# The third copy of probabilities on ScalarE, moved behind the second exponentials in dense heads that have a next one

## The chip, the core and the metric

The kernel runs on one core of one Trainium2 chip. The metric is the device time of one execution in microseconds; the time given is the median of the runs shown. Everything is computed in fp32, with matmuls of large operands split into a high and a low part.

## What is computed

A bidirectional encoder of two layers. Each layer projects its input (1,040 tokens, 1,024 channels) with `w_in`, runs three groups of mixers beside one another (a windowed attention A, two pairs of gated recurrences C0 and C1, four dense heads B0 to B3), projects with `w_out`, adds and normalises. The change lies in the dense heads, which are a differential attention:

```python
def attend(q_blk):                       # one block of 128 queries, c = 0, 1
    s = einsum('bqhcd,bkhcd->bhcqk', q_blk, k) * scale
    s = where(key_ok, s, NEG)
    p = softmax(s, axis=-1)
    a = p[:, :, 0] - lam * p[:, :, 1]
    return einsum('bhqk,bkhv->bqhv', a, v)
...
ob = rms_norm(ob, subln_w) * (1.0 - lam_init)
yb = ob * silu(gb)
```

Each head and query block has two score rows (c = 0 and 1) over 1,040 keys, two softmaxes, and a weighted difference that multiplies the values.

## The kernel before

All five engines run instruction streams written out by hand, which meet in semaphores; nothing schedules them but their order in the code. PSUM has eight banks, and `bank_plan` (line 240) gives every product its bank in advance. `filled` and `released` semaphores count the uses of each bank: `wait_filled` waits until TensorE has written a use, `wait_read` and `wait_free` until the reader has let it go.

The tokens are nine blocks: eight of 128 and the last, number 8, of the 16 meta tokens. Layer 0 needs all nine blocks as queries (`q_tiles` = 9), layer 1 eight.

The dense heads run in four passes a layer (`pass_b`, once for each engine: line 1100 for TensorE, 1431 for ScalarE, 1898 for VectorE), one pass a head, one step a query block. The passes of B0, B1 and B2 have a next head `nx`: its queries and keys are projected in halves of 12 matmuls between the work of the present head. B3 has none. The lists of `b_steps` (line 211) say which half products each step holds. In layer 0 the pass of B0 has two each in steps 0 and 1, one each in steps 2 to 5 and none in 6 to 8; those of B1 and B2 have two each in steps 0 to 5 and none in 6 to 8. In layer 1 the pass of B0 has two each in steps 0 to 2, one in 3 and 4, none in 5 to 7; those of B1 and B2 have three each in steps 0 and 1, two in 2 to 4, none in 5 to 7.

A step t of a pass goes like this. `after` is the next step, which at the end of a head is the first one of the next head.

- TensorE (lines 1151 to 1168): the scores of `after` into banks 2 to 5 (line 996), a wait for the combination of t, nine transposes of the combined p in three groups of three (line 1127; groups 0 and 2 into bank 0, group 1 into bank 1), a half product behind groups 0 and 1 and one behind group 2 if there are any (line 856), the values for key blocks 0 to 5, the values for blocks 6 to 8 (line 1143, into bank 1). The values for blocks 6 to 8 wait for the third copy. In the last step but one of a pass with a next head the meta scores of the next head follow (line 1085, matmuls of line 996).
- ScalarE (lines 1477 to 1497): two copies of transposed p out of PSUM, `evac_probs` 0 and 1 (line 1451), the exponentials of `after` for c = 0 (`exps`, a small one at line 1439 and the large one at line 1441, which also frees the score banks), the third copy `evac_probs` 2 (line 1451), the exponentials for c = 1, the output of the values (`values_out`, line 1461), and the normalisation (lines 1468 to 1472). In some steps a copy of rotated queries and keys of the next head stands among them (`qk_hi_of`, line 1419): that of pieces 0 and 1 ahead of the first exponentials, that of the last piece, in the last step but one, just ahead of the second.
- VectorE (lines 1942 to 1957): the maxima of `after` for c = 0 and 1 (lines 1906 and 1907), low parts of the next head (`qk_lo`, line 1881), its rotary work (`qk_rope`, lines 1867 to 1873), the end of the step before (`finish`), and the combination of `after` (`combine`, lines 1916 to 1922), which needs both exponentials.
- SyncE moves rotated pieces and saves results; GpSimd splits weights beside a maximum.

What the numbers in the prediction rest on is this order and three waits of the code:

```python
pe.wait_ge(b_comb, B_STEP[l, g, t])               # 1153, before the transposes
wait_read(pe, ("aT", l, g, t, k // 3))            # 1141, before values 0, 3, 6
pe.wait_ge(qk_lo_done, QK_PIECE[l, g, "qk", len(T_PIECES) - 1])   # 1088, meta scores
```

Scores also wait for their banks, that is for the exponentials of the step before (line 1111).

Of the kernel before, what the change touches and what calls it, by code (L numbers as in the profile page):

```python
# [62 lines left out]
def rows(t):  # L63
    return META if t == MT else P


def q_tiles(l):

    return TILES if l < DEPTH - 1 else REAL
# [141 lines left out]
def b_steps(l, nx):  # L211


    n = q_tiles(l)
    halves = [(u, half) for u in (units(l, nx, "qk") if nx else []) if u not in early(nx) for half in range(2)]
    q, r = divmod(len(halves), n - 3)
    ends = [(t + 1) * q + min(t + 1, r) for t in range(n)]
    parts = [halves[a:b] for a, b in zip([0] + ends, ends)]
    turned = [[]] + [[u for u, half in p if half] for p in parts[:-1]]
    rounded = [[] for _ in range(n)]  # L220
    rounded[0] += [j for f, j in early(nx) if f]
    for t in range(n):
        for f, j in turned[t]:
            if f:
                rounded[min(t + 2, n - 2)].append(j)
    return [(t, parts[t], turned[t], rounded[t]) for t in range(n)]
# [7 lines left out]
def b_step(l, g, t, k):  # L234
    steps = [(h, u) for h in B_HEADS for u in range(q_tiles(l))]
    i = steps.index((g, t)) + k
    return steps[i] if 0 <= i < len(steps) else None
# [183 lines left out]
def build(nc, x, meta, emb_ln_g, emb_ln_b, w_in, w_out, a_sink, b_lam, c_lb_logits, norm_cols,  # L421
# [177 lines left out]
    def slot_of(g):  # L599
        return (head_no(g) + 1) % 2  # L600

    def bank(key):
        return BANK[key][0]
# [6 lines left out]
    def wait_filled(eng, key):  # L610
        b, n = BANK[key]
        eng.wait_ge(filled[b], n + 1)

    def wait_read(eng, key):
        b, n = BANK[key]
        eng.wait_ge(released[b], n + 1)
# [584 lines left out]
    def _(act):  # L1201
        n_sca = [0]

        def then(ins):
            n_sca[0] += 1
            ins.then_inc(sca, 1)
            act.wait_ge(sca, n_sca[0])

        def hi_of_rows(what, l, t):
            for j in range(2):  # L1210
                key = (what, l, t, j)
                wait_filled(act, key)
                nc.scalar.copy(h_rows(hT_hi, j, t),
                               psum[:, bank(key), :].rearrange("p (k c) -> p k c", k=4)[:, :, 0:rows(t)]).then_inc(hi_split, 1)
# [201 lines left out]
        def qk_hi_of(l, g, j):  # L1416
            a, n = T_PIECES[j]
            act.wait_ge(qk_placed, 16 * 4 * QK_PIECE[l, g, "qk", j])
            nc.scalar.copy(qk_b[:, slot_of(g), 0:2, a:a + n], qk_t[:, :, 0:n]).then_inc(qk_hi, 1)

        def meta_out(l, g):
            for c in range(2):
                key = ("meta", l, g, c)
                n = q_tiles(l)
                wait_filled(act, key)
                if n == TILES:
                    nc.scalar.copy(meta_s[0:META, slot_of(g), c, MT, :], psum[0:META, bank(key), MT * META:TILES * META])
                nc.scalar.copy(meta_s[:, slot_of(g), c, 0:REAL, :].rearrange("p t m -> p (t m)"),
                               psum[:, bank(key), 0:REAL * META]).then_inc(released[bank(key)], 1)

        def pass_b(l, g, nx):
            def exps(step, c):
                g, t = step
                n = B_STEP[l, g, t]
                m, i = rows(t), n % 2
                act.wait_ge(b_max, B_COMP[l, g, t, c])
                b = bank(("s", l, g, t, c))
                probs = p0_b[0:m, i] if c == 0 else p1_b[0:m]
                nc.scalar.activation(probs[:, REAL * P:TOK], meta_s[0:m, slot_of(g), c, t, :], ACT.Exp, scale=SCALE,
                                     bias=neg_max[0:m, i, c:c + 1], accum_out=row_sum[0:m, i, 2 * c + 1:2 * c + 2])  # L1440
                nc.scalar.activation(probs[:, 0:REAL * P].rearrange("p (i n) -> p i n", i=2), psum[0:m, b:b + 2, :],  # L1441
                                     ACT.Exp, scale=SCALE, bias=neg_max[0:m, i, c:c + 1],
                                     accum_out=row_sum[0:m, i, 2 * c:2 * c + 1]).then_inc(released[b], 1)

            def evac_probs(t, j):
                key = ("aT", l, g, t, j)
                b, m = bank(key), rows(t)
                wait_filled(act, key)
                if b_step(l, g, t, -1) and j == 0:
                    wait_filled(act, ("o", l, *b_step(l, g, t, -1)))  # L1450
                nc.scalar.copy(aT_b[:, 3 * j:3 * j + 3, 0:m],  # L1451
                               psum[:, b, 0:3 * P].rearrange("p (k c) -> p k c", k=3)[:, :, 0:m])\
                    .then_inc(released[b], 1)

            def values_out(t):
                key = ("o", l, g, t)
                n, b = B_STEP[l, g, t], bank(key)
                wait_filled(act, key)
                if n > 2:
                    act.wait_ge(b_y, n - 2)  # L1460
                nc.scalar.copy(o_b[0:rows(t), n % 2, :], psum[0:rows(t), b, 0:P]).then_inc(released[b], 1)

            def norm(step):
                g, t = step
                n, m = B_STEP[l, g, t], rows(t)
                wait_read(act, ("o", l, g, t))
                act.wait_ge(b_scale, n)
                then(nc.scalar.activation(b_junk[0:m, :], o_b[0:m, n % 2, :], ACT.Square,
                                          accum_out=sumsq[0:m, t, 0:1]))
                then(nc.scalar.activation(rstd[0:m, t, 0:1], sumsq[0:m, t, 0:1], ACT.Ln, bias=eps_rms[0:m],  # L1470
                                          scale=fscale[0:m, n % 4, :]))
                nc.scalar.activation(rstd[0:m, t, 0:1], rstd[0:m, t, 0:1], ACT.Exp, scale=-0.5).then_inc(rstd_ready, 1)

            if g == "B0":
                exps((g, 0), 0)
                exps((g, 0), 1)
            for t, _, _, before in b_steps(l, nx):
                after = b_step(l, g, t, 1)
                evac_probs(t, 0)
                evac_probs(t, 1)  # L1480
                for j in before:
                    if j < len(T_PIECES) - 1:
                        qk_hi_of(l, nx, j)
                if after:
                    exps(after, 0)
                evac_probs(t, 2)
                for j in before:
                    if j == len(T_PIECES) - 1:
                        qk_hi_of(l, nx, j)
                if after:  # L1490
                    exps(after, 1)
                values_out(t)
                norm((g, t))
                if nx and t == q_tiles(l) - 2:
                    meta_out(l, nx)
                if not nx and t >= Y_LAG:
                    hi_of_rows("y", l, t - Y_LAG)
# [5 lines left out]
        for l in range(DEPTH):  # L1503
# [32 lines left out]
            for g, nx in b_passes(l):  # L1536
                pass_b(l, g, nx)
# [526 lines left out]
```

## Time and profile before

| | |
|---|---|
| median of 3 runs | 1895.43 us (1888.45 to 1899.31) |
| the profiled execution | 1886.95 us, span 1885.6 us |
| granted TensorE clock, mean | 0.965 of full speed |
| busy: TensorE | 1707.6 us (91%) |
| busy: VectorE | 1100.9 us (58%) |
| busy: ScalarE | 886.8 us (47%) |
| busy: GpSimd | 402.9 us (21%) |
| chain that ended last | TensorE 70%, VectorE 16%, ScalarE 6% |

The busy shares are means over stages with different limits. The dense heads take some 300 us in each layer (562 to 858 and 1481 to 1776 us of the span). A timeline row gives the start, the length, the engine, the line, the operation with what it writes and reads, and in brackets the idle time of the engine before it and what ended it. Matmuls are pipelined, so their rows overlap: the distance of two starts says more than a length.

### The profile page before, as it was taken

Reading aid. Unit: us, or ns where it says so; the run is one execution under the profiler, and the core shown is the slowest. Engines: PE = TensorE matmul, PEld = TensorE weight load, DVE = VectorE, ACT = ScalarE, POOL = GpSimd, SP = SyncE. Lnnn points to the kernel's source line nnn. Section 1 sums busy time; section 2 is a strip of 40 time slices with the busy share of each in tenths; the row PEclk is TensorE's granted clock in tenths of the full one; section 3 lists DMA queues with packets and bytes.
Section 4 is the critical chain, followed back from the end, with each engine's and each line's share of the span. In section 5 each row is a group of like instructions: output and inputs, shape, how many; then the busy total and the mean of one; then the engine's idle time right before and its main releaser. Section 6 shows DMA issues by size and latency. Waiting matters only on the chain.

```text
span 1885.6 us, 35772 instructions
## 1 busy us (share of the span) xinstructions
PE 1707.6 (91%) x13754; PEld 1584.6 (84%) x13754; DVE 1100.9 (58%) x2533; ACT 886.8 (47%) x2652; POOL 402.9 (21%) x390
## 2 busy tenths in 40 slices
PE   3799999999998999989989989999998898888896
PEld 2798899999887788768989989999998878776796
DVE  6585584345537777783185845834453575667616
ACT  4434545345506666682063344452553374647603
POOL 5430221220111002011373103113103001012044
PEclk9999999999989999899999999999998999899998
DMA  7200100200020111142121001012001111103312
GB/s 256 69 24 13 57 23 27 77 23 13 32 78 15 38 31 38 46 143 96 37 103 53 24 14 56 23 34 70 26 13 59 50 29 31 47 22 128 121 46 90
DMA packets 97705, 102.44 MB, mean 54 GB/s; under 512 B 7488, under 2 KB 87600, under 8 KB 97280
## 3 DMA queue, kind: packets, MB, share of 16 engines
q1 hardware_dynamic: 96576, 99.08, 16.3%
q8 instruction: 111, 1.82, 0.4%
q10 hardware_dynamic: 960, 1.07, 0.2%
q14 instruction: 58, 0.48, 0.1%
HBM read 70.43 MB, written 21.17 MB: 49 GB/s over the span
## 4 chain that ended last, share of the span: by engine, by line
PE 70%; DVE 16%; ACT 6%; POOL 3%; issue 2%; DMA 2%; SPq 0%; DVEq 0%; ACTq 0%
PE psum L856 45%; PE psum L996 7%; PE psum L931 3%; PE psum L1143 3%; PE psum L1050 3%; DVE row_max L1906 3%; PE psum L1127 2%; ACT p_b L1441 2%; DVE p_b L1920 2%; PE psum L1036 1%; POOL w_lo L822 1%; PE psum L903 1%; ACT aT_b L1451 1%; PE psum L979 1%; PE psum L974 1%
## 5 line engine op out<-in xcount | busy, mean ns | idle before, releaser
L856 PE MATMUL psum<-w_hi,hT_hi 128*128 128x256 f32 x1824 | 529.2, 290 | 6.2 <-POOL w_lo L822 4.3
L856 PE MATMUL psum<-w_hi,hT_lo 128*128 128x256 f32 x1824 | 516.6, 283 | 0.0
L856 PE MATMUL psum<-w_lo,hT_hi 128*128 128x256 f32 x1824 | 516.3, 283 | 0.0
L818 POOL CAST w_hi<-w_raw 128x512 fp32r<-128x512 f32 (+1 forms) x168 | 109.6, 652 | 1319.4 <-DMA w_raw<-in_w_in 791.5
L856 PEld LDWEIGHTS psum<-w_hi,hT_hi 128*128 128x128 f32 x1824 | 347.6, 191 | 14.8 <-POOL w_lo L822 5.1
L856 PEld LDWEIGHTS psum<-w_hi,hT_lo 128*128 128x128 f32 x1824 | 347.5, 191 | 0.0
L856 PEld LDWEIGHTS psum<-w_lo,hT_hi 128*128 128x128 f32 x1824 | 347.4, 190 | 0.0
L856 PE MATMUL psum<-hT_hi,w_hi 128*128 128x346 f32 (+1 forms) x672 | 229.8, 342 | 24.6 <-DVE hT_lo L1565 9.3
L856 PE MATMUL psum<-hT_hi,w_lo 128*128 128x346 f32 (+1 forms) x672 | 220.9, 329 | 0.0
L856 PE MATMUL psum<-hT_lo,w_hi 128*128 128x346 f32 (+1 forms) x672 | 220.6, 328 | 0.0
L822 POOL TENSOR_TENSOR w_lo<-w_raw,w_hi 128x512 fp32r<-128x512 f32 (+1 forms) x168 | 211.4, 1258 | 25.9 <-DVE neg_max L1907 14.1
L1906 DVE TENSOR_REDUCE row_max<-psum 128x1 f32<-128x1024 f32 x136 | 165.8, 1219 | 54.5 <-PE psum L996 54.5
L1143 PE MATMUL psum<-vg_b,aT_b 128*128 128x128 f32 (+1 forms) x1224 | 164.9, 288 | 5.0 <-ACT aT_b L1451 4.4
L996 PE MATMUL psum<-qk_b 64*128 64x512 f32 (+2 forms) x1224 | 144.4, 372 | 22.6 <-ACT p_b L1441 18.1
L1143 PEld LDWEIGHTS psum<-vg_b,aT_b 128*128 128x128 f32 (+1 forms) x1224 | 149.5, 192 | 13.7 <-ACT aT_b L1451 8.5
L856 PEld LDWEIGHTS psum<-hT_hi,w_hi 128*128 128x128 f32 x672 | 131.3, 195 | 27.0 <-issue 10.0
L1441 ACT ACTIVATE p_b<-psum,neg_max 128x1024 f32<-128x1024 f32 x136 | 149.9, 1102 | 0.0
L996 PEld LDWEIGHTS psum<-qk_b 64*128 64x128 f32 (+1 forms) x1224 | 101.3, 193 | 46.0 <-issue 25.0
L1451 ACT COPY aT_b<-psum 128x384 f32<-128x384 f32 (+1 forms) x204 | 88.2, 464 | 108.2 <-PE psum L1127 106.2
L856 PEld LDWEIGHTS psum<-hT_hi,w_lo 128*128 128x128 f32 x672 | 131.4, 196 | 0.0
L856 PEld LDWEIGHTS psum<-hT_lo,w_hi 128*128 128x128 f32 x672 | 130.7, 194 | 0.0
L1127 PEld LDWEIGHTS psum<-ident,p_b 128*128 128x128 f32 (+1 forms) x612 | 70.9, 149 | 64.0 <-DVE p_b L1920 30.8
(161 smaller groups left out, 2618.6 us busy)
## 6 DMA issues: line engine op xcount, KB each, us to landing
w_raw<-in_w_in SPq DMA_DIRECT2D x72, 256.0 KB, 3.5
w_raw<-in_w_in SPq DMA_DIRECT2D x28, 512.0 KB, 4.2
h_dram<-hbuf SPq DMA_DIRECT2D x16, 512.0 KB, 2.6
w_raw<-in_w_out SPq DMA_DIRECT2D x16, 512.0 KB, 4.1
hbuf<-h_dram SPq DMA_DIRECT2D x16, 512.0 KB, 5.9
qk_b<-y_dram SPq DMA_DIRECT2D x16, 512.0 KB, 3.2
y_dram<-y_stage SPq DMA_DIRECT2D x96, 64.0 KB, 1.6
qk_t<-rot SPq DMA_DIRECT2D x56, 86.5 KB, 2.1
```

What stands on the lines that cost most here:

```text
L818: pool.tensor_copy(hi, raw).then_inc(w_hi_done, 1)
L822: pool.tensor_tensor(lo, raw, hi.bitcast(F32), ALU.subtract).then_inc(w_split, 1)
L856: last = nc.tensor.matmul(out_ap, lhs[a](k), rhs[b](k), start=k == 0 and a + b == 0, stop=k == KT - 1 and b == 1)
L931: last = nc.tensor.matmul(o_ap, k_sel[p0:p0 + HD, a:a + m], q_ap, start=True, stop=True)
L996: last = [nc.tensor.matmul(out_of(r), q_of(a, r), k_of(b, r), start=i == 0, stop=i == 2) for r in range(2)]
L1050: last = nc.tensor.matmul(psum[0:m, bank(o_key), h * HD:(h + 1) * HD], pT_a[:, h % 2, j, 0:m], v_a[:, f + j - 1 if j else MT, v0:v0 + HD], ...
L1127: last = nc.tensor.transpose(psum[:, b, i * P:i * P + m], p0_b[0:m, B_STEP[l, g, t] % 2, k * P:(k + 1) * P], ident[0:m, 0:m])
L1143: last = nc.tensor.matmul(psum[0:m, b, 0:P], aT_b[:, k, 0:m], vg_b[:, head_no(g), k, 0:P], start=k == 0, stop=k == TILES - 1)
L1441: nc.scalar.activation(probs[:, 0:REAL * P].rearrange("p (i n) -> p i n", i=2), psum[0:m, b:b + 2, :], ACT.Exp, scale=SCALE, bias=neg_max[ ...
L1451: nc.scalar.copy(aT_b[:, 3 * j:3 * j + 3, 0:m], psum[:, b, 0:3 * P].rearrange("p (k c) -> p k c", k=3)[:, :, 0:m])\
L1906: then(nc.vector.tensor_reduce(row_max[0:m, i, c:c + 1], psum[0:m, b:b + 2, :], AX.XY, ALU.max))
L1920: stt(p0_b[0:m, i, 0:TOK], p1_b[0:m, :], coef[0:m, j, 0:1], p0_b[0:m, i, 0:TOK], ALU.mult, ALU.add).then_inc(b_comb, 1)
```

## The change

In a pass that has a next head, the third copy of the transposed probabilities (`evac_probs(t, 2)`) is issued after the exponentials for c = 1 of the next step instead of between those for c = 0 and c = 1. In the pass of B3 it stays where it was.

```diff
@@ -1483,12 +1483,16 @@
                         qk_hi_of(l, nx, j)
                 if after:
                     exps(after, 0)
-                evac_probs(t, 2)
+                if not nx:
+                    evac_probs(t, 2)
                 for j in before:
                     if j == len(T_PIECES) - 1:
                         qk_hi_of(l, nx, j)
                 if after:
                     exps(after, 1)
+                if nx:
+
+                    evac_probs(t, 2)
                 values_out(t)
                 norm((g, t))
                 if nx and t == q_tiles(l) - 2:
```

On ScalarE a common step of such a pass, before (p_b is the buffer of probabilities, aT_b that of the transposed ones):

```order
L1451 COPY aT_b<-psum 128x384 x2
L1439 ACTIVATE p_b,row_sum<-meta_s,neg_max 128x16
L1441 ACTIVATE p_b,row_sum<-psum,neg_max 128x1024
L1451 COPY aT_b<-psum 128x384
L1439 ACTIVATE p_b,row_sum<-meta_s,neg_max 128x16
L1441 ACTIVATE p_b,row_sum<-psum,neg_max 128x1024
L1461 COPY o_b<-psum 128x128
```

and with the change:

```order
L1451 COPY aT_b<-psum 128x384 x2
L1439 ACTIVATE p_b,row_sum<-meta_s,neg_max 128x16
L1441 ACTIVATE p_b,row_sum<-psum,neg_max 128x1024
L1439 ACTIVATE p_b,row_sum<-meta_s,neg_max 128x16
L1441 ACTIVATE p_b,row_sum<-psum,neg_max 128x1024
L1451 COPY aT_b<-psum 128x384
L1461 COPY o_b<-psum 128x128
```

The copy of 128x384 that stood between the two pairs of exponentials now stands behind both, just ahead of the output of the values.

The last step but one of a pass, on ScalarE (here in the pass of B0 in layer 0, where `after` has 16 rows), before:

```order
L1451 COPY aT_b<-psum 128x384 x2
L1439 ACTIVATE p_b,row_sum<-meta_s,neg_max 16x16
L1441 ACTIVATE p_b,row_sum<-psum,neg_max 16x1024
L1451 COPY aT_b<-psum 128x384
L1419 CAST qk_b<-qk_t 128x2x346
L1439 ACTIVATE p_b,row_sum<-meta_s,neg_max 16x16
L1441 ACTIVATE p_b,row_sum<-psum,neg_max 16x1024
L1461 COPY o_b<-psum 128x128
```

and with the change:

```order
L1451 COPY aT_b<-psum 128x384 x2
L1439 ACTIVATE p_b,row_sum<-meta_s,neg_max 16x16
L1441 ACTIVATE p_b,row_sum<-psum,neg_max 16x1024
L1419 CAST qk_b<-qk_t 128x2x346
L1439 ACTIVATE p_b,row_sum<-meta_s,neg_max 16x16
L1441 ACTIVATE p_b,row_sum<-psum,neg_max 16x1024
L1451 COPY aT_b<-psum 128x384
L1461 COPY o_b<-psum 128x128
```

The copy of rotated queries and keys (line 1419) now follows the first exponentials at once, and the third copy has moved behind two instructions more. The rows of TensorE, VectorE, GpSimd and SyncE stand as before.

## Rows read from the trace of the kernel before

**Rows 1.** The waits, whole run: engine line <- releaser: us in total, times, longest us
```profile
PEld psum L1127 <- DVE p_b L1920: 30.8, 31, 2.9
```

**Rows 2.** Timeline, a full step (B1, layer 0): start us, us, engine, line, operation
```profile
659.85 0.88 PE L1127 MATMUL psum<-ident,p_b 128*128 128x128 f32 x6
...
659.96 1.22 DVE L1906 TENSOR_REDUCE row_max<-psum 128x1 f32<-128x1024 f32 x1 [1.50 <-PE psum L996]
...
661.41 0.31 ACT L1439 ACTIVATE p_b<-meta_s,neg_max 128x16 f32<-128x16 f32 x1
...
662.54 0.29 DVE L1907 SCALAR_TENSOR_TENSOR neg_max<-row_max,meta_max 128x1 f32<-128x1 f32 x1
...
664.70 2.17 PE L1143 MATMUL psum<-vg_b,aT_b 128*128 128x128 f32 x18
...
666.81 1.67 PE L996 MATMUL psum<-qk_b 64*128 64x512 f32 x12
...
668.40 0.87 PE L1127 MATMUL psum<-ident,p_b 128*128 128x128 f32 x6
...
668.50 1.23 DVE L1906 TENSOR_REDUCE row_max<-psum 128x1 f32<-128x1024 f32 x1 [1.20 <-PE psum L996]
```

**Rows 3.** Timeline, half steps 3 and 4 of B0, layer 0
```profile
597.36 0.87 PE L1127 MATMUL psum<-ident,p_b 128*128 128x128 f32 x6 [0.62 <-DVE p_b L1920]
...
598.73 0.31 ACT L1439 ACTIVATE p_b<-meta_s,neg_max 128x16 f32<-128x16 f32 x1
...
600.87 0.31 ACT L1439 ACTIVATE p_b<-meta_s,neg_max 128x16 f32<-128x16 f32 x1
...
604.48 0.87 PE L1127 MATMUL psum<-ident,p_b 128*128 128x128 f32 x6 [0.32 <-DVE p_b L1920]
...
611.86 0.87 PE L1127 MATMUL psum<-ident,p_b 128*128 128x128 f32 x6 [0.32 <-DVE p_b L1920]
```

**Rows 4.** Timeline, bare steps 5 and 6 of B0, layer 1
```profile
1533.35 0.87 PE L1127 MATMUL psum<-ident,p_b 128*128 128x128 f32 x6 [0.32 <-DVE p_b L1920]
...
1538.47 0.15 DVE L1916 TENSOR_TENSOR inv_sum<-row_sum 128x2 f32<-128x2 f32 x1
...
1540.47 0.88 PE L1127 MATMUL psum<-ident,p_b 128*128 128x128 f32 x6 [0.69 <-DVE p_b L1920]
...
1541.85 0.31 ACT L1439 ACTIVATE p_b<-meta_s,neg_max 128x16 f32<-128x16 f32 x1
...
1543.24 0.46 ACT L1451 COPY aT_b<-psum 128x384 f32<-128x384 f32 x1
...
1543.60 0.77 ACT L1419 CAST qk_b<-qk_t 128x692 fp32r<-128x692 f32 x1
...
1543.76 0.94 PE L1143 MATMUL psum<-vg_b,aT_b 128*128 128x128 f32 x6 [0.18 <-ACT aT_b L1451]
...
1544.27 0.31 ACT L1439 ACTIVATE p_b<-meta_s,neg_max 128x16 f32<-128x16 f32 x1
...
1545.34 2.85 PE L996 MATMUL psum<-qk_b 64*128 64x16 f32 x48 [0.65 <-DVE qk_b L1881]
```

**Rows 5.** Timeline, bare step 7 of B0, layer 1
```profile
1553.41 0.32 ACT L1439 ACTIVATE p_b<-meta_s,neg_max 128x16 f32<-128x16 f32 x1
...
1555.02 0.16 DVE L1916 TENSOR_TENSOR inv_sum<-row_sum 128x2 f32<-128x2 f32 x1 [1.94 <-ACT p_b L1441]
...
1557.03 0.88 PE L1127 MATMUL psum<-ident,p_b 128*128 128x128 f32 x6 [0.30 <-DVE p_b L1920]
```

**Rows 6.** Stretches, end of B2, layer 0: length, busy PE PEld DVE ACT POOL, PEclk, DMA, GB/s
```profile
775.00:780.00 5.00, 3.09 (x25) 1.65 (x24) 4.65 (x13) 2.74 (x9) 0.00 (x0) 1.00 0.32 72
...
785.00:790.00 5.00, 5.00 (x44) 4.45 (x44) 2.38 (x10) 0.74 (x5) 0.00 (x0) 0.50 0.01 4
```

**Rows 7.** The chain of waits, meta scores and scores at two head ends: start us, us
```profile
630.94 4.93 PE psum L996 x66
...
783.55 7.03 PE psum L996 x51
```

## The prediction

> **What bounds the kernel now.** I write a step of a dense head as the time from T, the start of TensorE's first six transposes of p (line 1127), to the next such start. The change acts in the 51 steps that have a next head: 27 of layer 0, 24 of layer 1. I split them by how many half products of the next head's queries and keys TensorE has in them, as the lists of `b_steps` give it: 27 *full* steps (two or three), 6 *half* steps (one: steps 2 to 5 of B0 in layer 0, steps 3 and 4 of B0 in layer 1), and 18 *bare* steps (none: the last three of each of six passes). Read first the waits: TensorE's weight load before the transposes waits for VectorE's combination 31 times [rows 1]. That is under half of the 68 steps of both layers, so most steps are bound by TensorE and some by the softmax chain. Then I read the timeline of one step of each kind.
>
> Full step [rows 2]: transposes at 659.85 (the step before it ended there), next at 668.40, 8.55 us, with no wait printed on TensorE. The reader is to see that the second maximum is out at 662.83 (662.54+0.29) and that the values begin at 664.70 and the next scores at 666.81.
>
> Half step [rows 3]: 597.36 to 604.48, 7.12 us. First exponentials start at 598.73 (T+1.37), second at 600.87, and TensorE then waits for line 1920.
>
> Bare steps [rows 4]: 1533.35 to 1540.47, also 7.12 us; the next one ends in the meta scores at 1545.34, which wait for the low parts (line 1881). The last step of a head [rows 5] goes from the second exponentials (1553.41) by the combination (1555.02) to the next transposes (1557.03).
>
> **The change, part by part.** One copy of 128x384 (line 1451) moves behind one pair of exponentials. No instruction is added, none removed, no DMA is touched, and TensorE, VectorE, GpSimd and SyncE keep their order. What moves is who comes first on ScalarE. Behind it three things hang: the last three matmuls of the values (k = 6 to 8), bank 0, and by TensorE's own order the next scores or the meta scores. The normalisation follows the values and is late with them, but VectorE asks for it only behind the two maxima of the next step, and SyncE for the result only after that.
>
> *Gain.* Between the start of the copy and the start of what follows it lie 0.36 us (1543.24 to 1543.60) [rows 4]. Where the copy also waited for TensorE's transposes, as in the half step, the second exponentials can start at T+1.37+1.39 = T+2.76 instead of T+3.51: 0.75 us earlier. The 1.39 is what one pair of exponentials holds ScalarE (1541.85 to 1543.24) [rows 4].
>
> *Cost.* From the start E of the second exponentials there are two ways to the next transposes. By the combination: 1.61 + 2.01 = E+3.62 [rows 5]. By TensorE, new: the copy starts at E+1.39, the last values 0.52 later (1543.24 to 1543.76) [rows 4], they take a third of 664.70 to 666.81, 0.70, and the scores 1.59 (666.81 to 668.40) [rows 2]. That is E+4.20. So once the copy stands behind the exponentials, TensorE's way is the longer by 0.58 us, and what E gains must first pay for that. Also, if scores and not the combination set T, the first maximum starts 0.10 behind T (668.40, 668.50), and the first exponentials 1.45 behind the maximum (659.96 to 661.41) [rows 2]: at T+1.55 instead of T+1.37.
>
> By kind:
> - Full steps, 27: ScalarE is free at 661.41+1.39 = 662.80 and the maximum is there at 662.83; the copy then starts at 664.22, and block 6 is ready at 664.74. TensorE comes to it after twelve of eighteen matmuls, at 664.70+1.40 = 666.10 [rows 2]. Slack 1.4 us, or 0.7 where a copy of 0.67 (line 1419) comes first. Nothing changes: 0. The earlier combination is worth nothing either, since no TensorE instruction of the step waits for it; if the cover of 1.4 us were gone, each such step would pay the overrun.
> - Half steps, 6: after the first, T+1.55+1.39+4.20 = T+7.14 against 7.12, so 0.02 each. The two with a copy of line 1419 ahead: 1.37+0.67+1.39+4.20 = 7.63 against 604.48 to 611.86, 7.38 [rows 3]: +0.25 each. Together +0.6.
> - First bare step of a head, 6: the combination starts at 1538.47 with no idle time printed ahead of it [rows 4], so VectorE's own rotary work holds it either way and the step keeps its length; only in B0, where the half steps before have shifted the maximum by 0.18, it moves: 2 x 0.18 = +0.4.
> - Second bare step, 6, up to the meta scores. Before: 1540.47 to 1545.34 = 4.87. After: 1.37+1.39 = 2.76 the copy of line 1419, +0.67 the second exponentials, +1.39 the moved copy, +0.52+0.70 the values, so the meta scores at 6.04. The low parts, which ended the wait before, would be ready earlier and no longer matter. +1.17 each, and meta scores, scores and maximum follow one another without a gap, so it goes to the end: +7.0.
> - Third bare step, 6: E is 0.36 earlier, then 4.20 instead of 3.62: +0.22 each [rows 4, 5], +1.3.
> - The first step of B3, unchanged in itself, inherits the late maximum: 2 x 0.17 = +0.3.
>
> Sum +9.6 us.
>
> *The clock*, which the steps above take as full. After the bare steps of B2 in layer 0 TensorE, busy 3.09 of 5 us, has 1.00 granted at first, then 0.50 in 785 to 790 (the level of 1.2 GHz), and the meta scores with the scores take 7.03 us there against 4.93 at the end of B0 [rows 6, 7]. The change adds idle time just ahead of that place in six heads. Bounds: nothing, if none of the six is slower than before, and 6 x 2.1 = 12.6. I take one more slow crossing, 2.1, since of the two crossings shown one is slow already [rows 7].
> The Trainium skill, page "TensorE: Matmul & The Clock Gate", section "Loop structure matters more than you think", says that another engine copying a result out of PSUM doesn't break the clock. By that rule this term is nil and the sum is 9.6; the rows speak against relying on it, since the clock fell in a stretch where TensorE's waits are of just this sort.
>
> Total +11.7, say +12. The profiled execution took 1886.95 us, 8.5 below the median of the three runs; both move by the same sum, so 1899 for such an execution and **1907.4 us** for the median.
>
> **The rivals.**
> - *The clock carries it.* The added idle makes most of the six crossings run at half clock: 9.6 + 12.6 = +22, 1917.6 us. For it: the two levels and their prices [rows 6, 7]. Against: stretches of bare steps now stay at 1.00 for several us.
> - *Half of it is hidden.* If the meta scores' delay is taken up behind them (the last step of a head waits for its own maxima too), half of the 7.0 goes: +6, 1901 us, not to be told from no change, since under about 0.5% (9.5 us) a measurement of this kernel sees nothing. Against: the transposes of that step follow the scores at once.
> - *The earlier combination wins*, the other side. Place: half and bare steps. If TensorE's way from E were no longer than 3.62, each gets what E gains: 4 x 0.75 and 2 x 0.36 in half steps, 6 x 0.36 in third bare steps, 6 x 0.36 at the meta scores, in all 8.1 us less, 1887.3; up to -10 if the rotary steps gain. It decides where the copy starts before E+0.81 instead of E+1.39. Against it: ScalarE is in order and a pair holds it 1.39 us. For it: only that a trace's waits are inferred.
> - *The copy in full steps is late.* With 0.3 us over in each it would be +8 more. Against: the slack of 1.4.
>
> **How the numbers follow.** Forecast (+9.6 to +14): 0.50, of which 0.10 falls under 9.5. Clock: 0.15. Half hidden, some +3 to +8: 0.25, of which 0.02 over the line. Combination wins: 0.10, half of it beyond 0.5%. The late copy in full steps is counted with the clock case. Slower 0.57, same 0.38, faster 0.05. The range from 1897 (+2) to 1920 (+25) leaves out the winning combination and what is beyond six slow crossings.
>
> **What would show it.** Right: in bare steps the copy of line 1451 starts 1.39 behind the second exponentials, TensorE's wait for it before the last values grows to about 1 us and more, the waits for line 1920 before the transposes nearly vanish, the meta scores start 6.0 behind T and wait for the values, and full steps stay at 8.55. Wrong: if full steps grow, if half steps fall under 7.0, or if the meta scores still wait for line 1881.

## The result, and the profile after

The changed kernel took 1922.95 us (median of 4 runs, 1919.51 to 1929.96), the kernel before 1892.93 us (4 runs). The ratio is 1.016 with a 95% interval of 1.0131 to 1.0189: 30 us slower, where +12 was forecast and 1920 (+25) was the end of the range. When it was measured once more it was 1.0149 (1.0125 to 1.0173). The profiled execution took 1929.96 us and is the slowest of its four, while that of the kernel before (1886.95 us) is faster than all of its four; so the two traces lie 43 us apart, not 30.

The page of the changed kernel (busy times; the granted clock in 40 slices; the chain by engine):

```profile
span 1928.6 us, 35772 instructions
...
PE 1733.7 (90%) x13754; PEld 1602.8 (83%) x13754; DVE 1099.4 (57%) x2533; ACT 888.7 (46%) x2652; POOL 403.3 (21%) x390
...
PEclk9899999999989898899999999999998899898998
...
PE 72%; DVE 14%; ACT 8%; POOL 2%; issue 2%; DMA 2%; SPq 0%; DVEq 0%; ACTq 0%
```

TensorE has 26 us more of busy time for the same 13,754 matmuls: they ran slower, not more often. The stage table says where; 12.8 and 4.7 us of the 26 lie in its second and fourth rows. It cuts the span at the first transposes of the dense heads and at those of B3, in each layer; the columns are the length, the busy times of PE, PEld, DVE, ACT and POOL with their counts, the granted clock, the DMA share and GB/s. Before:

```profile
0.00:572.61 572.61, 505.19 (x4215) 477.89 (x4215) 315.37 (x791) 246.17 (x754) 134.49 (x133) 0.97 0.18 57
572.61:797.20 224.59, 210.42 (x1601) 182.90 (x1599) 169.90 (x377) 149.95 (x453) 25.94 (x27) 0.95 0.12 32
797.20:1491.85 694.65, 649.25 (x5357) 612.64 (x5357) 377.05 (x875) 289.48 (x870) 165.75 (x162) 0.98 0.17 55
1491.85:1721.72 229.87, 204.86 (x1466) 181.79 (x1465) 153.69 (x332) 135.88 (x399) 25.86 (x27) 0.92 0.12 32
1721.72:1885.60 163.88, 137.90 (x1120) 129.38 (x1120) 84.85 (x162) 65.33 (x176) 50.88 (x41) 0.96 0.29 103
```

After:

```profile
0.00:579.39 579.39, 510.83 (x4214) 483.66 (x4214) 316.14 (x791) 246.47 (x754) 134.51 (x133) 0.96 0.18 56
579.39:821.57 242.18, 223.21 (x1602) 191.50 (x1600) 170.12 (x376) 150.23 (x453) 25.98 (x27) 0.90 0.12 32
821.57:1519.39 697.82, 652.25 (x5359) 614.21 (x5358) 374.26 (x874) 289.97 (x870) 165.96 (x162) 0.97 0.17 54
1519.39:1764.58 245.19, 209.60 (x1466) 184.23 (x1464) 154.05 (x331) 136.60 (x399) 25.92 (x27) 0.91 0.11 31
1764.58:1928.60 164.02, 137.85 (x1122) 129.17 (x1120) 84.85 (x161) 65.45 (x176) 50.93 (x41) 0.96 0.29 102
```

The reader is to see the second and fourth rows, the passes that the change touches: 224.59 to 242.18 us and 229.87 to 245.19 us, +32.9 together, at a granted clock of 0.95 to 0.90 and 0.92 to 0.91. (In layer 1 the mean clock hardly differs, because the trace of before was slow in other places of that row; the steps below say more.) The other three rows, which hold the same instructions in the same order, are 10.1 us longer in this pair of executions (6.8 of it ahead of the first dense head). The first row differs so without the change too: full_steps_only, below, has 578.69 us there in its profiled execution and is no slower than the kernel before.

The waits of the changed kernel that answer to [rows 1] come second; the first line is from the kernel before:

```profile
PEld psum L1143 <- ACT aT_b L1451: 8.5, 18, 1.0
```

```profile
PEld psum L1143 <- ACT aT_b L1451: 43.8, 31, 2.6
...
PEld psum L1127 <- DVE p_b L1924: 17.1, 17, 2.9
...
PE psum L996 <- DVE qk_b L1885: 0.9, 2, 0.5
```

The wait before the transposes fell from 30.8 us in 31 cases to 17.1 in 17. Of these 17, 11 lie in the passes of B3, which the change leaves alone (13 before); elsewhere it fell from 18 cases to 6. In its place stands the wait of the values for the third copy, 43.8 us in 31 cases where it was 8.5 in 18. The meta scores wait for the low parts (line 1881, now 1885) in two places only.

A half step after, step 3 of B0 in layer 0, to be held against [rows 3]:

```profile
605.29 0.87 PE L1127 MATMUL psum<-ident,p_b 128*128 128x128 f32 x6
...
606.81 0.31 ACT L1439 ACTIVATE p_b<-meta_s,neg_max 128x16 f32<-128x16 f32 x1
...
608.28 0.31 ACT L1439 ACTIVATE p_b<-meta_s,neg_max 128x16 f32<-128x16 f32 x1
...
609.67 0.47 ACT L1451 COPY aT_b<-psum 128x384 f32<-128x384 f32 x1
...
610.19 0.94 PE L1143 MATMUL psum<-vg_b,aT_b 128*128 128x128 f32 x6 [0.46 <-ACT aT_b L1451]
...
611.05 1.65 PE L996 MATMUL psum<-qk_b 64*128 64x512 f32 x12
...
612.64 0.87 PE L1127 MATMUL psum<-ident,p_b 128*128 128x128 f32 x6
```

First exponentials at T+1.52, second at T+2.99 (T+3.51 before), the copy 1.39 behind them, the last values 0.52 later, the scores 0.86 later, the next transposes 1.59 later: 7.35 us against 7.12. A full step keeps its length, and its values have no wait:

```profile
682.08 0.87 PE L1127 MATMUL psum<-ident,p_b 128*128 128x128 f32 x6
...
686.49 0.47 ACT L1451 COPY aT_b<-psum 128x384 f32<-128x384 f32 x1
...
686.91 2.17 PE L1143 MATMUL psum<-vg_b,aT_b 128*128 128x128 f32 x18
...
690.61 0.87 PE L1127 MATMUL psum<-ident,p_b 128*128 128x128 f32 x6
```

The second bare step of B0 in layer 1, with what follows (to be held against [rows 4, 5]):

```profile
1568.23 0.87 PE L1127 MATMUL psum<-ident,p_b 128*128 128x128 f32 x6
...
1569.78 0.31 ACT L1439 ACTIVATE p_b<-meta_s,neg_max 128x16 f32<-128x16 f32 x1
...
1571.83 0.31 ACT L1439 ACTIVATE p_b<-meta_s,neg_max 128x16 f32<-128x16 f32 x1
...
1573.23 0.47 ACT L1451 COPY aT_b<-psum 128x384 f32<-128x384 f32 x1
...
1573.74 0.94 PE L1143 MATMUL psum<-vg_b,aT_b 128*128 128x128 f32 x6 [2.41 <-ACT aT_b L1451]
...
1574.61 7.10 PE L996 MATMUL psum<-qk_b 64*128 64x16 f32 x60
...
1581.64 1.28 PE L1127 MATMUL psum<-ident,p_b 128*128 128x128 f32 x6
...
1586.63 0.94 PE L1143 MATMUL psum<-vg_b,aT_b 128*128 128x128 f32 x6 [1.54 <-ACT aT_b L1451]
```

The meta scores start 6.38 us behind T, where they started at 4.87. Then the meta scores and scores take 7.03 us to the next transposes (1574.61 to 1581.64), where they took 4.36 (1545.34 to 1549.70). So this step is 4.18 us longer, 1.51 by the wait and 2.67 by slower matmuls.

The prediction calls the meta scores with the scores behind them a *crossing*, from one head to the next. TensorE is busy without a break in it, so its length shows the clock alone. In layer 0 it has 66 matmuls. Here is that of B2 in the kernel before, in the changed kernel, and in full_steps_only (below), where this step has the order of the kernel before:

```profile
783.55:790.49 6.94, 6.94 (x66) 5.90 (x66) 3.57 (x15) 2.10 (x11) 0.00 (x0) 0.59 0.03 9
804.76:812.82 8.06, 8.06 (x68) 7.01 (x67) 1.92 (x10) 1.80 (x9) 0.00 (x0) 0.50 0.00 0
792.56:796.91 4.35, 4.35 (x66) 3.81 (x67) 3.14 (x13) 2.10 (x11) 0.00 (x0) 1.00 0.05 15
```

The same work takes 4.35 us at full clock and 8.06 at half. The six crossings together take 32.4 us in the kernel before, at granted clocks of 0.59 to 0.97, and 45.0 us in the changed one, at 0.50 to 0.60. At full clock throughout they would take 25.9 (three of 4.35 and three of 4.27 us).

### The profile page after: what moved, and what is told of

It is laid out like the page before. It is cut to its first block, busy times and chain, and to the rows that moved or that the text cites. A ratio compares the mean times of both kernels' runs of the same rounds, so it can differ in the third digit from the quotient of the medians.

```text
span 1928.6 us, 35772 instructions
## 1 busy us (share of the span) xinstructions
PE 1733.7 (90%) x13754; PEld 1602.8 (83%) x13754; DVE 1099.4 (57%) x2533; ACT 888.7 (46%) x2652; POOL 403.3 (21%) x390
## 4 chain that ended last, share of the span: by engine, by line
PE 72%; DVE 14%; ACT 8%; POOL 2%; issue 2%; DMA 2%; SPq 0%; DVEq 0%; ACTq 0%
PE psum L856 44%; PE psum L996 9%; PE psum L1143 4%; PE psum L931 3%; ACT p_b L1441 3%; DVE row_max L1910 3%; PE psum L1050 3%; PE psum L1127 2%; PE psum L1036 1%; DVE hbuf L1583 1%; ACT aT_b L1451 1%; PE psum L903 1%; DVE stats L1576 1%; ACT p_b L1439 1%; POOL w_lo L822 1%
## 5 line engine op out<-in xcount | busy, mean ns | idle before, releaser
L1143 PEld LDWEIGHTS psum<-vg_b,aT_b 128*128 128x128 f32 (+1 forms) x1224 | 147.8, 189 | 49.5 <-ACT aT_b L1451 43.8
L996 PE MATMUL psum<-qk_b 64*128 64x512 f32 (+2 forms) x1224 | 165.1, 410 | 14.1 <-ACT p_b L1441 13.2
L996 PEld LDWEIGHTS psum<-qk_b 64*128 64x128 f32 (+1 forms) x1224 | 115.9, 228 | 41.0 <-issue 19.3
```

The costliest lines, as they stand in the source:

```text
L996: last = [nc.tensor.matmul(out_of(r), q_of(a, r), k_of(b, r), start=i == 0, stop=i == 2) for r in range(2)]
L1143: last = nc.tensor.matmul(psum[0:m, b, 0:P], aT_b[:, k, 0:m], vg_b[:, head_no(g), k, 0:P], start=k == 0, stop=k == TILES - 1)
```

## The experiments

Two theories stood against one another. The **wait theory**: a wait costs its length, as in the prediction's sum. The **clock theory**: the longer idle time of TensorE at the end of a pass brings the granted clock down to 0.50 over the meta scores and scores, and most of the loss is that. The table has the length of the six *meta steps* in each kernel's trace (second bare step, from transposes to transposes), in the order B0, B1, B2 of layer 0, then of layer 1. Each row of six comes from one traced execution, while the median comes from 4 to 12 runs. Each ratio is to the kernel before measured beside it, whose medians were 1891.58 to 1894.06 us after the first one of 1892.93:

| kernel | six meta steps, us | sum | median, us | ratio to before, 95% |
|---|---|---|---|---|
| before | 9.69 10.46 11.77 9.23 10.76 9.64 | 61.6 | 1892.93 | |
| changed | 13.51 13.92 14.43 13.41 14.10 13.96 | 83.3 | 1922.95 | 1.0160 (1.0131 to 1.0189) |
| changed_again | 13.50 14.12 14.63 13.55 14.31 14.20 | 84.3 | 1923.36 | 1.0149 (1.0125 to 1.0173) |
| full_steps_only | 11.47 10.64 9.19 9.73 9.65 9.93 | 60.6 | 1892.78 | 0.9993 (0.9977 to 1.0009) |
| only_meta_step | 12.37 12.77 13.18 12.53 14.90 13.21 | 79.0 | 1909.41 | 1.0091 (1.0059 to 1.0123) |
| all_but_meta_step | 11.00 11.86 11.62 10.56 11.72 11.93 | 68.7 | 1909.11 | 1.0081 (1.0053 to 1.0109) |
| filled_wait | 10.60 13.49 10.99 10.66 10.51 12.56 | 68.8 | 1910.86 | 1.0093 (1.0063 to 1.0124) |
| filled_wait_again | 10.60 13.50 10.98 13.26 10.82 10.81 | 70.0 | 1918.55 | 1.0136 (1.0115 to 1.0158) |
| filled_wait_nine | 10.61 11.11 12.94 10.66 11.33 11.22 | 67.9 | 1907.64 | 1.0086 (1.0065 to 1.0108) |
| bare_steps_filled | 11.96 11.73 11.38 10.63 10.64 13.29 | 69.6 | 1907.59 | 1.0094 (1.0069 to 1.0120) |
| only_meta_filled | 10.94 12.91 10.52 11.65 12.21 12.08 | 70.3 | 1908.11 | 1.0083 (1.0061 to 1.0104) |
| only_meta_filled_nine | 10.92 10.52 11.55 12.14 10.48 10.49 | 66.1 | 1902.19 | 1.0051 (1.0032 to 1.0069) |
| high_parts_first | 9.78 10.51 11.89 9.59 9.45 9.72 | 60.9 | 1893.15 | 1.0006 (0.9993 to 1.0019) |
| before_filled | 11.38 10.57 9.19 9.92 10.05 10.18 | 61.3 | 1893.51 | 1.0015 (1.0000 to 1.0030) |

A single step says little: that of B2 in layer 0, with the order of the kernel before, took 11.77, 9.19, 11.89 and 9.19 us in four of these kernels. The sums of six with that order and nothing moved near them agree: 61.6, 60.6, 60.9 and 61.3.

### Which of the moves cost: full_steps_only, only_meta_step, all_but_meta_step

In the kernel before, `late` says in which steps the copy moves:

```diff
+                late = nx and len(halves) > 1             # full_steps_only
+                late = nx and t == q_tiles(l) - 2         # only_meta_step
+                late = nx and t != q_tiles(l) - 2         # all_but_meta_step
-                evac_probs(t, 2)
+                if not late:
+                    evac_probs(t, 2)
...
                     exps(after, 1)
+                if late:
+                    evac_probs(t, 2)
```

> The copy is moved only in the 27 steps with two or three half products. Both theories: TensorE reaches the last values 1.4 us after the copy is done, so nothing, 1893 within 0.3%. If the copy were late in full steps, each would be longer than 8.55 us and this kernel slower by more than 5 us.

Measured: 0.9993. The 27 full steps cost nothing, as the slack in [rows 2] said, and the rival of a late copy in full steps is out.

> The third copy is moved only in the step that ends in the meta scores (6 steps), 45 of the moves are undone. Wait theory (an added wait costs its length and no more): +7.0 us by the prediction's sum, near 1900. Clock theory (the wait ahead of the meta scores leaves them, and what follows, at half clock): the six steps now cost 21.8 us and the steps behind them some 4 more, so +20 to +26 us, 1913 to 1919, and the meta step is 13.5 us long in layer 0 against 9.7.

Measured: 1.0091, 17 us for six moves, where the waits alone should have made 7. The six steps take 79.0 us in place of 61.6, which is those 17 us. Half of it, 8.7 us, lies in the crossings (41.1 us in place of 32.4); the other half is the later start of the meta scores, 1.32 to 1.36 us in five of the six steps and not 1.17.

> The copy is moved in 45 steps and stays between the exponentials in the six that end in the meta scores. Wait theory: +2.6 us, no change that can be told, 1896. Clock theory: the meta scores start without the long wait, so most crossings keep the clock they have in the kernel before: +3 to +8 us, 1896 to 1901. If the idle time of the bare steps in general is what lowers the clock, the crossings stay slow and it comes out at +15 or more, 1908.

Measured: 1.0081, 15 us for 45 moves that should have made 2.6. This was above what either theory had named, and at the level that the expectation gave for idle time of the bare steps in general. In the trace the first and third bare steps are 3.8 and 2.9 us longer, the half steps 1.4. The six meta steps have the order of the kernel before, and yet they are 7.1 us longer in sum: 1.1 us before the meta scores start, 6.0 us in the crossings (38.4 us in place of 32.4). The second one of them (length, busy times, granted clock 0.75):

```profile
712.63:724.49 11.86, 10.82 (x93) 9.11 (x93) 7.06 (x21) 6.35 (x21) 0.00 (x0) 0.75 0.10 24
```

So matmuls ran slower in steps whose own order is unchanged. More idle time ahead of them is not the reason: the meta step and the step ahead hold 20.3 us of TensorE's idle time over the six heads, and 20.2 and 20.3 in full_steps_only and high_parts_first. What differs is how it is spread. The waits of the first bare step of B2 in layer 0, in the kernel before and then in all_but_meta_step:

```profile
774.54 0.94 PE L1143 MATMUL psum<-vg_b,aT_b 128*128 128x128 f32 x6 [0.82 <-ACT aT_b L1451]
...
776.03 1.57 PE L996 MATMUL psum<-qk_b 64*16 64x512 f32 x12 [0.55 <-ACT p_b L1441]
...
778.72 0.88 PE L1127 MATMUL psum<-ident,p_b 128*128 128x128 f32 x6 [1.12 <-DVE p_b L1920]
```

```profile
788.09 0.94 PE L1143 MATMUL psum<-vg_b,aT_b 128*128 128x128 f32 x6 [2.20 <-ACT aT_b L1451]
...
790.87 0.88 PE L1127 MATMUL psum<-ident,p_b 128*128 128x128 f32 x6 [0.36 <-DVE p_b L1924]
```

Three waits of 0.82, 0.55 and 1.12 us have become one of 2.20 and one of 0.36, and the step is as long as before (8.09 us). That the long wait is what lowers the clock in the next step is argued from this; no run varies it alone. Both halves of the change lose by themselves, and their losses add up to about the whole (17 + 15 against 30).

### Filling the wait with work: filled_wait, filled_wait_again, filled_wait_nine, changed_again

The changed kernel, with products added that nobody reads, ahead of the last values in the six meta steps. They go to the bank that the meta scores overwrite next. Only work is added.

```diff
+                if nx and t == q_tiles(l) - 2:
+                    for c in range(2):
+                        wait_free(pe, ("meta", l, nx, c))
+                    for _ in range(7):                    # 9 in filled_wait_nine
+                        nc.tensor.matmul(psum[0:rows(t), bank(("meta", l, nx, 0)), 0:P], aT_b[:, 0, 0:rows(t)],
+                                         vg_b[:, head_no(g), 0, 0:P], start=True, stop=True)
                 values(t, range(6, TILES))
```

> The changed kernel with seven products of values added in the six meta steps, written into the bank of the meta scores while TensorE waits for the third copy: 1.6 us of work inside a wait of 2.2 us, whose results nobody reads. Wait theory: the work is hidden and the time stays at the changed kernel's 1923. Clock theory: the meta scores and scores keep full clock, 4.9 us instead of 6.9, in six places, and it comes down by 10 to 15 us, 1908 to 1913.

Measured: 1910.86, 12 us below the changed kernel with more work to do. Two of the six meta steps stayed slow, 13.49 and 12.56 us. The meta step of B0 in layer 1: before, then changed, then filled_wait.

```profile
1540.47:1549.70 9.23, 8.16 (x87) 6.83 (x87) 6.74 (x17) 6.29 (x19) 0.00 (x0) 0.98 0.12 30
```

```profile
1568.23:1581.64 13.41, 10.76 (x90) 9.11 (x88) 6.83 (x17) 6.46 (x19) 0.00 (x0) 0.78 0.09 21
```

```profile
1555.88:1566.54 10.66, 9.56 (x103) 8.42 (x101) 6.83 (x17) 6.46 (x19) 0.00 (x0) 1.00 0.11 28
```

The three clocks are 0.98, 0.78 and 1.00, the lengths 9.23, 13.41 and 10.66 us. At full clock the change costs this step 1.43 us; what lies above that, 2.75 us, is the clock at its lower level of 1.2 GHz for part of the step.

> filled_wait once more, with more rounds, since only_meta_filled did not gain as it should. Clock theory: again 10 us or more below the changed kernel's 1923, 1907 to 1913. Wait theory: 1923.

Measured: 1918.55, 1.0136 (1.0115 to 1.0158). That is only 4 us below the changed kernel's median, where ten were expected, and the intervals overlap: a miss. Its trace has two slow meta steps (13.50 and 13.26 us), as the one of filled_wait had; why the medians differ by 8 us is not shown. Seven products do not keep the clock reliably.

> The changed kernel itself, beside the next one on the same chip, since the two fillings of seven came to 1910.9 and 1918.6 in different jobs. Both theories: 1.016 of the kernel before, 1920 to 1926, and 13 to 14.5 us for each meta step.

> The changed kernel with nine products of values as filler in the wait of the six meta steps, 2.1 us at full clock in a wait of 2.2. Wait theory: equal to changed_again. Clock theory: at least 8 us below changed_again, 1906 to 1914, and at least four of the six meta steps at 10.5 to 11 us with a granted clock of 0.95 or more. What then remains over the kernel before, 13 to 20 us, is the waits themselves (12 us by the steps at full clock) and slow stretches in the other bare steps.

These two ran on the same chip. Measured: 1923.36, with meta steps of 13.50 to 14.63 us, and 1907.64. Nine products in each of six waits make the kernel 15.7 us faster. All six meta steps are shorter than in changed_again, by 16.4 us in sum. But only two of them, not four, came to 10.5 to 11 us at a clock of 0.95 or more; the other four were granted 0.93, 0.76, 0.93 and 0.94, so this part of the expectation was wrong. The steps of B0 in layer 1 and of B2 in layer 0, the fast one and the one that stays slow:

```profile
1554.23:1564.89 10.66, 10.01 (x108) 8.87 (x106) 6.82 (x17) 6.46 (x19) 0.00 (x0) 1.00 0.11 28
788.49:801.43 12.94, 12.77 (x114) 10.97 (x112) 7.14 (x20) 6.54 (x21) 0.00 (x0) 0.76 0.07 19
```

### Filling elsewhere: only_meta_filled, only_meta_filled_nine, bare_steps_filled, before_filled

The first two are only_meta_step with the same filler of seven and of nine products.

> The copy is moved only in the six meta steps, and the wait that this makes is filled with seven products of values that nobody reads. Wait theory: the filler changes nothing, so it stays at the 1909.4 of the unfilled one. Clock theory: with full clock over the meta scores what is left is the wait itself, 6 x 1.2 = +7, 1900 to 1902, and the meta steps are 10.6 us long in layer 0.

Measured: 1908.11 against 1909.41, no gain that can be told, though in the profiled executions the six steps went from 79.0 to 70.3 us. A miss of the clock theory as put. In five of the six the clock is still under 1, here the fourth:

```profile
1555.56:1567.21 11.65, 10.73 (x102) 9.09 (x102) 6.74 (x17) 6.40 (x19) 0.00 (x0) 0.89 0.10 25
```

> The copy moved in the six meta steps alone and nine products as filler instead of seven, 2.1 us at full clock in a wait of 2.2. With seven it came to 1908.1 against 1909.4 without any, and the granted clock in five of the six steps was still 0.80 to 0.95. Clock theory: with the wait closed the steps come near 10.6 us and the time to 1902 or less. If it stays at 1908, the filler inside this wait is not what decides here, and the idle time of the steps ahead sets the clock; in filled_wait those steps are in the other order.

Measured: 1902.19, 1.0051 (1.0032 to 1.0069). With the wait closed the loss is 9.6 us instead of the 17 of the unfilled kernel, and four of six steps are at 10.5 to 10.9. So the filler does decide here, and seven were too few; against only_meta_filled alone the intervals still touch.

bare_steps_filled is the changed kernel with fillers of five, seven and six products in the three bare steps, each ahead of the last values. `idle_work` issues that many of the same products, into a free bank that `spare` names.

```diff
+                if nx and t >= q_tiles(l) - 3:
+                    idle_work(t, {3: 5, 2: 7, 1: 6}[q_tiles(l) - t], spare(t))
                 values(t, range(6, TILES))
```

> The changed kernel with fillers of five, seven and six products in the three bare steps of a pass, all inside the waits for the third copy. Wait theory: 1923, as without. Clock theory: filled_wait came to 1910.9 with two of six crossings still slow (13.5 and 12.6 us); with the steps around filled as well all six are fast, so +10 to +12 over the kernel before, 1904, which is the sum of the waits alone in the prediction.

Measured: 1907.59, the ratio 1.0094. It falls against 1923 as the clock theory says, but not to 1904, and only two of the six meta steps are fast (10.63 and 10.64 us at a clock of 1.00); one is still 13.29. It does no better than filled_wait (1.0093), which has the same seven products in the meta steps and none elsewhere, so the filler in the other bare steps brought nothing that can be told.

before_filled is the kernel before with two products in each of three waits at a pass's end: ahead of the transposes of the second bare step, and after the values of the first and of the second (there ahead of the meta scores).

```diff
                 scores(b_step(l, g, t, 1))
+                if nx and q_tiles(l) - 2 <= t < q_tiles(l) - 1:
+                    idle_work(t, 2, spare(t))
...
                     project(l, nx, "qk", x, half)
+                if nx and q_tiles(l) - 3 <= t <= q_tiles(l) - 2:
+                    idle_work(t, 2, spare(t))
```

The expectation speaks of four waits; the diff has these three.

> The kernel before, its order kept, with two products of values that nobody reads in each of four waits at the end of a pass with a next head: ahead of the scores, twice, ahead of the transposes and ahead of the meta scores. Wait theory: no change, 1893. Clock theory: the meta steps, 9.2 to 11.8 us long before, all come to 9.2 to 9.7, 4 to 5 us less in all, 1889, which five rounds can just tell.

Measured: 1893.51, 1.0015. No gain; if anything a loss. TensorE's idle time in the meta steps and the ones ahead fell to 11.0 us over the six heads (16.5 in the trace of before), and yet the meta steps stayed at 61.3 us, with clocks of 0.79 to 1.00. Waits of 0.65 to 1.12 us in the kernel before are not worth filling this way, and the expectation of 4 to 5 us was wrong. So the clock doesn't follow the sum of idle time in and just ahead of the step.

### The other order: high_parts_first

The kernel before with one swap, the copy of line 1419 ahead of the third copy, both ahead of the second exponentials.

```diff
                 if after:
                     exps(after, 0)
-                evac_probs(t, 2)
                 for j in before:
                     if j == len(T_PIECES) - 1:
                         qk_hi_of(l, nx, j)
+                evac_probs(t, 2)
```

> The kernel before with one swap in the six meta steps: the copy of the last rotated piece comes ahead of the third copy, and the third copy stays ahead of the second exponentials. By the rows, the high parts are out 0.36 us earlier, the low parts would let the meta scores start at T+4.5 and the last values at T+4.65 (before: 4.87). Wait theory: -0.2 us a place, no change that can be told, 1891 to 1893, and the meta scores wait for the values and no more for the low parts. Clock theory: the same, since TensorE idles no longer than before. If the mere swap lowered the clock it would show as +5 or more.

Measured: 1.0006 (0.9993 to 1.0019), no change, as expected. The meta scores start at T+4.82 (T+4.87 in the kernel before), not at the T+4.65 of the expectation. The wait has moved to the values, 0.85 us of it, at the place of [rows 4]:

```profile
1548.64 0.76 ACT L1419 CAST qk_b<-qk_t 128x692 fp32r<-128x692 f32 x1
...
1549.30 0.47 ACT L1451 COPY aT_b<-psum 128x384 f32<-128x384 f32 x1
...
1549.83 0.94 PE L1143 MATMUL psum<-vg_b,aT_b 128*128 128x128 f32 x6 [0.85 <-ACT aT_b L1451]
```

It was the only order tried that might have been faster than both kernels, and it is not.

## Why the prediction was wrong, point by point

In short: the waits cost about what was forecast, 11 to 12 us for 9.6. The rest, some 18 us, are matmuls that ran at the lower clock, where the prediction had put 2.1.

- *Which steps pay, and which way.* Right. Full steps are free (0.9993), half and bare steps lose, the copy starts 1.38 to 1.40 us behind the second exponentials, the waits for line 1920 gave way to waits for line 1451, and the meta scores wait for the low parts in two places only. The forecast was slower, and it is slower.
- *The way by TensorE, E+4.20.* Mis-sized a little. Measured 4.36 in the half step (608.28 to 612.64). The three last values took 0.86 us until the scores started and not 0.70, a third of the 2.11 of a run without a break. In that run itself the last third took 0.76 (666.04 to 666.81, by single matmuls), so 0.06 is the division by three and 0.10 comes of the wait. The late maximum was counted in some steps and left out in others (the first exponentials of the meta step stood at T+1.55, not 1.37).
- *The sum of the waits, +9.6.* Mis-sized by some 2. By the steps that ran at full clock: half steps +1.4 (0.23, 0.39, 0.16, 0.27, 0.38), first bare steps of B0 2 x 0.18 = +0.4, meta steps 6 x 1.33 to 1.43 = +8.0 to +8.6 (9.19 in full_steps_only to 10.52 in only_meta_filled, B2 of layer 0; 9.23 to 10.66 for B0 of layer 1), third bare steps 3 x 0.28 in layer 0 (7.03 in full_steps_only to 7.30 to 7.32 in the filled kernels) and 3 x 0.05 in layer 1 (7.32 to 7.36 to 7.38) = +1.0, B3's first step 0.07 and 0.18 = +0.3. That makes +11.1 to +11.7, an estimate from these steps. The largest error in it is the meta step, 1.33 to 1.43 for 1.17.
- *The clock, "I take one more slow crossing, 2.1".* This is the step that failed. Not one more crossing was slow but all six, at clocks of 0.50 to 0.60: 45.0 us in place of 32.4, which is 12.6 us. Slow stretches came up in other bare steps too: the first ones are 3.9 us longer in sum and the third ones 5.1, where waits account for 0.4 and 1.0 (8.88 us for 6.71 in the last step of B1 in layer 0, 9.30 for 7.91 in the first bare step of B1 in layer 1). The difference of 30 less the 11 to 12 of the waits leaves some 18 us for the clock, and filling six waits gave back 15.7.
- *Where that term came from.* The price was wrong too. The 4.93 us taken for a crossing at full clock had a granted clock of 0.88, and the 7.03 taken for a slow one had 0.59; the two levels are 4.35 and 8.06. And of the six crossings of the kernel before only two were read: the others had 0.74, 0.97, 0.70 and 0.88, so all six were already partly slow. That the bound of 6 x 2.1 = 12.6 equals what the crossings gained is luck; as a bound on the whole term it was too low, since it left out the steps around.
- *The rule weighed there.* The Trainium skill, "TensorE: Matmul & The Clock Gate", section "Loop structure matters more than you think", says of VectorE's copy out of PSUM that it doesn't break the clock, in a loop whose next matmuls follow immediately. The prediction left that condition out. The runs agree with the Trainium skill where its condition holds: in the full steps TensorE has other work beside the copy, and moving it there cost nothing (0.9993). In the meta steps TensorE waits for the copy, so the rule doesn't speak of them: the clock was 0.78 over a step whose longest wait was 2.41 us. The prediction also said that TensorE's waits in the stretch of [rows 6] are of just this sort. Of the four longer ones there, 0.82, 0.55, 1.12 and 0.65 us, only the first is for a copy of transposed p out of PSUM.
- *The rivals.* "The clock carries it", +22 us with a chance of 0.15, was the one that came true, short by 8 of the 30. (Its 1917.6 us is nearer, 5 us off, only because it was added to 1895.43 and the kernel before came to 1892.93 with a fourth run.) What I held against it, that bare steps stay at full clock for several us, was read from stretches whose waits were under 1.2 us. The earlier combination (whose terms add to 8.0 and not 8.1), a half-hidden meta step and a late copy in full steps are all out: the copy starts at E+1.39, the third bare step behind a fast meta step doesn't get shorter (7.32 to 7.38 us for B0 of layer 1), and full_steps_only is no slower.
- *Open.* How much idle time it takes is not settled: seven products failed to hold the clock in some places, nine held it better but not everywhere (0.76 in one step), and two measurements of the same filled kernel differ by 8 us. Nor is it shown why the crossings of all_but_meta_step are slow. Nor was the mere swap of TensorE's scores ahead of the last values tried.

## What to carry to other kernels

When a copy moves behind longer work on an engine that keeps the order of the code, as ScalarE did here, follow the reader of that copy in its own engine's order: here the last values stood ahead of the next scores, so second exponentials that started 0.2 to 0.6 us earlier (0.52 in the half step shown) bought nothing, and the scores paid. Price a new wait on TensorE twice, once as its length and once as the matmuls behind it at the lower clock, and look in the granted clock of every stretch of the kind for places where it already falls. Here all six crossings were partly slow before (0.59 to 0.97), and all six were slow after (0.50 to 0.60). A wait can be tested for this without touching the order: put useless products into it and see whether the kernel gets faster.

## What was not expected of the hardware

- Adding 54 products that nobody reads made the kernel 15.7 us faster (1923.36 to 1907.64).
- Six steps with unchanged order became 7.1 us longer in sum, 6.0 of it by slower matmuls, when only the steps around them were changed (all_but_meta_step), though TensorE's idle time in and just ahead of them was no longer than in full_steps_only (20.3 and 20.2 us).
- The values of three key blocks take 0.86 us until the next product starts when they follow a wait (610.19 to 611.05), against 0.76 in a stream.
